# Weighted values of an attention block: the hi and lo weights moved in one 512-column matmul, with a sum of three pieces on VectorE

## The chip, the cores and the metric

The kernel runs on one core of one Trainium2 chip. The metric is the device time of one execution in microseconds (us). The engines are named as in the profile: PE is TensorE, with PEld for its weight loads, DVE is VectorE, ACT is ScalarE, POOL is GpSimd and SP is SyncE, which issues the DMAs.

## What is computed

One decoder layer over 1024 tokens of width 1024: half a SwiGLU feed-forward block (inner width 2816), a token mixer, and half a second feed-forward block, each behind an RMS norm and added to x, then a final norm. The change lies in the mixer, which has 8 stick-breaking heads and 8 dilated sliding-window heads of size 64:

```python
# stick-breaking head
z = q @ k.T * scale; mask = key < query
log_stay = where(mask, log_sigmoid(-z), 0)
later = reverse_cumsum(log_stay) - log_stay
weights = where(mask, exp(log_sigmoid(z) + later), 0)
out = weights @ v
# dilated head: softmax over z in each pattern, patterns mixed by their denominators, then weights @ v
```

What matters here is the last product, weights times v, of all 16 heads. All of it is float32.

## The kernel before, in words

**Precision.** Every float32 operand of a large product is split in two: hi is the value rounded to the reduced format in which PE takes float32 data (F32R), lo is what the rounding left. A product is then hi·hi + hi·lo + lo·hi. ACT writes the hi parts (a copy into an F32R tile) and DVE or POOL the lo parts (value minus hi).

**The stages.** `ffn_block` (first feed-forward), `heads_block` (projections and attention), `output_block` (the mixer's output projection) and `ffn_block` again. The change is in `heads_block` alone.

**The heads block.** It works in runs: four pairs of heads (`PAIRS`), and for each first the stick-breaking kind (`SB_KIND`) and then the dilated kind (`DIL_KIND`), eight runs in all. A run has 8 steps s: step s works on head s // 4 of the pair and on query group g = s % 4, which is 256 queries (`QG`). Group g looks at keys up to its own last one, so it has 2(g + 1) key tiles of 128. Runs sit in a loop on each engine (`Fori`) for the first three pairs; the last pair is written out, and its last run has no projection work beside it, because there is no further pair to project.

**What each engine does in a step.** The order on each engine is written out by hand in its `step` function:
- PE: the scores of the next step (`scores`, L1130 to L1161, into four PSUM banks); then, for each turn j of g + 1, some units of the next pair's projections (`project`, L1124 to L1126, as many as the table `UNITS` says), the transposes of the weights of two key tiles (`turn_weights`, L1180, into one bank of two), and the weighted values of the turn that lies two turns back (`values_behind` and `weighted_values`, L1194 to L1208).
- ACT: gates or exponentials (L819, L820, L829) of the next step, the hi part of the turned weights (`weights_hi`, L846), and where a step's values are complete, the copy of their lower half into `o_low` (`values_low`, L886). It also takes projections out of their bank (L861, L863, L867).
- DVE: scans or masked maxima (L956, L968), the normalising of the dilated weights (`normalize`, L981 and L983), the lo part of the turned weights (`weights_lo`, L997), rotations (L1032, L1035, L1041), and `values_out` (L1015).
- POOL: the stick-breaking products (`products`, L739), which end the making of a step's weights for that kind, one part of the rotations, and lo parts of the projection weights.

**The weighted values.** `v_both` holds for each key tile and head 128 columns: 64 with the hi part of v, 64 with the lo part. They are PE's stationary operand, so a matmul gives 128 rows: v_hi·w in rows 0 to 63 and v_lo·w in rows 64 to 127. Each key tile takes two matmuls with the same stationary operand and the same output columns of bank 4 (`BANK_PV`), one with `wt_hi` (L1206) and one with `wt_lo` (L1207). Both move 256 columns, except for the last key tile of a group, of which only 128 queries look at it, so that both move 128. Over all runs there are 256 tiles of the first kind and 64 of the second.

**How the bank is handed back.** There is one bank for it. When the last matmul of step s is done (`pv_ready`), ACT copies rows 64 to 127 of the bank into `o_low` (L886), DVE adds `o_low` to rows 0 to 63 and writes the sum into `o_stage` (L1015), in partitions 0 to 63 for the first head of the pair and 64 to 127 for the second. Only then (`o_copied`) may PE start the weighted values of step s + 1:

```python
if j == 0:
    pe.wait_ge(o_copied, 1 + STEPS * run(it, kind) + s)     # L1200
...
dve.wait_ge(o_low_done, STEPS * run(it, kind) + s + 1)      # L1014
dve.tensor_tensor(o_stage[rows, g * QG:(g + 1) * QG], b.ps[0:HEAD, BANK_PV, 0:QG], o_low[:, :],
                  ALU.add).then_inc(o_copied, 1)            # L1015
```

There are 64 such hand-backs. On DVE, `values_out` of a step stands between `weights_lo` and the scan or the masked maximum for the step after next (L1059 to L1065). In steps with g = 1 it stands there twice: once for the step with g = 3 before, once for the step with g = 0.

Of the kernel before, what the change touches and what calls it, by code (L numbers as in the profile page):

```python
# [30 lines left out]
P = 128  # L31
# [552 lines left out]
def heads_block(nc, b, sem, norm, w_in, neg_mask, log_count, cos, sin, o_dram, w_out, group_gain):  # L584
# [3 lines left out]
    with ExitStack() as ctx:  # L588
# [5 lines left out]
        cos_sb, sin_sb = sb("cos", [P, SEQ]), sb("sin", [P, SEQ])  # L594
        log_count_sb = sb("log_count", [P, SEQ])
        neg_f = sb("neg_f", [P, P])
        wt_hi = sb("wt_hi", [P, TT, QG], F32R)
        wt_lo = sb("wt_lo", [P, TT, QG], F32R)
        o_stage = sb("o_stage", [P, SEQ])
        w_raw, w_hi, w_lo = [b.w_raw[:, i, :, :] for i in range(2)], b.w_hi, b.w_lo  # L600

# [26 lines left out]
        turned, turn_hi_done, turn_split = sem("turned"), sem("turn_hi_done"), sem("turn_split")  # L628
        out_w_loaded = [sem(f"out_w_loaded{i}") for i in range(2)]
        out_w_hi_done, out_w_gained, out_w_split = (sem(f"out_w_{n}") for n in ("hi_done", "gained", "split"))  # L630
        pv_ready, o_low_done, o_copied = sem("pv_ready"), sem("o_low_done"), sem("o_copied")
        o_stored = [sem(f"o_stored{h}") for h in range(2)]
        block = ctx.enter_context(nc.Block())

# [13 lines left out]
        def run(it, kind):  # L648
            return 2 * it + kind
# [299 lines left out]
        def _(dve):  # L949
# [58 lines left out]
            def values_out(it, kind, s):  # L1008

                head, g = s // 4, s % 4  # L1010
                rows = slice(head * HEAD, (head + 1) * HEAD)
                if g == 0:
                    dve.wait_ge(o_stored[head], 16 * (run(it, kind) + 1))
                dve.wait_ge(o_low_done, STEPS * run(it, kind) + s + 1)  # L1014
                dve.tensor_tensor(o_stage[rows, g * QG:(g + 1) * QG], b.ps[0:HEAD, BANK_PV, 0:QG], o_low[:, :],  # L1015
                                  ALU.add).then_inc(o_copied, 1)

# [91 lines left out]
        def _(pe):  # L1109
# [84 lines left out]
            def weighted_values(it, kind, s, j, v_turn):  # L1194


                head, g = s // 4, s % 4
                pe.wait_ge(turn_split, 1 + TURNS * run(it, kind) + turn_index(s, j, v_turn) + 1)
                if j == 0:
                    pe.wait_ge(o_copied, 1 + STEPS * run(it, kind) + s)  # L1200
                for kk in range(2):
                    k, part = 2 * j + kk, wt_part(s, j) + kk
                    end = k == 2 * g + 1
                    cols = slice(P, QG) if end else slice(0, QG)
                    out, v = b.ps[:, BANK_PV, cols], v_both[kind][:, k, head, :]
                    pe.matmul(out, v, wt_hi[:, part, cols], start=(k == 0), stop=False)  # L1206
                    last = pe.matmul(out, v, wt_lo[:, part, cols], start=False, stop=end)  # L1207
                last.then_inc(pv_ready, 1)  # L1208

            def values_behind(it, kind, s, j, n):  # L1210
# [393 lines left out]
```

## Time and profile before

| | us |
|---|---|
| median of 3 executions | 2274.57 |
| lowest, highest | 2273.68, 2276.44 |
| span of the profiled execution, first to last instruction | 2270.4 |
| PE busy in it | 2185.7 |
| DVE busy in it | 996.2 |
| ACT busy in it | 658.7 |
| POOL busy in it | 215.3 |

The profile comes from one execution of its own, of which it states the span and not the whole time; the median of the runs stands 4.2 us above that span. Busy times are unions of instructions on an engine. A matmul's record is longer than the time it holds the engine, since matmuls overlap in the pipeline: what one costs is read from the start of one to the start of the next. In rows of a timeline, the bracket at the end gives the engine's idle time in front of the instruction and what ended it.

### The profile page before, as it was taken

To read this page: it belongs to the slowest core of one execution; us is meant where nothing else is said; L and a number is where in the kernel's file an instruction comes from. 1 tells how busy PE (TensorE), PEld (TensorE's weight loads), DVE (VectorE), ACT (ScalarE), POOL (GpSimd) and SP (SyncE) were. 2 spreads that over 40 slices of the span, in tenths; PEclk is the share of its full clock that TensorE was granted. 3 is DMA by queue.
4 is the path that set the end of the run, shared out by engine and by line. 5 is a ranking of instruction groups with operands and counts; after the bars stand their busy time and mean duration, and the time that the engine had idled before them with its cause. 6 is when DMAs were issued, how large, how long until landed. Compare 5 with 4: busy or idle time off the path is not lost. (4 is left out here: it accounts for less than half of the span.)

```text
span 2270.4 us, 26317 instructions
## 1 busy us (share of the span) xinstructions
PE 2185.7 (96%) x10016; PEld 1785.8 (79%) x10016; DVE 996.2 (44%) x1578; ACT 658.7 (29%) x1143; POOL 215.3 (9%) x138
## 2 busy tenths in 40 slices
PE   7999999999999899999999997799999999999998
PEld 6888888888887677777777776687888888888887
DVE  4233333332334446566565656343333333333236
ACT  5211111111112344554544545332211111111112
POOL 0000000000000032141241235300000000000000
PEclk9999999999999999999989986899999999999999
DMA  4111110111110301010110112402111111011101
GB/s 168 56 56 55 55 45 11 55 55 55 56 38 28 111 25 43 15 49 31 30 39 23 33 38 66 171 1 84 56 56 56 55 55 55 4 51 55 56 19 74
DMA packets 37960, 118.51 MB, mean 52 GB/s; under 512 B 4865, under 2 KB 9217, under 8 KB 37889
## 3 DMA queue, kind: packets, MB, share of 16 engines
q1 hardware_dynamic: 37888, 117.61, 14.5%
q8 instruction: 40, 0.66, 0.1%
q14 instruction: 32, 0.25, 0.0%
HBM read 100.81 MB, written 12.58 MB: 50 GB/s over the span
## 5 line engine op out<-in xcount | busy, mean ns | idle before, releaser
L360 DVE TENSOR_TENSOR scaled_rows<-banks,scaled_rows 128x512 f32<-128x512 f32 x88 | 60.9, 692 | 665.4 <-PE banks L435 511.4
L997 DVE TENSOR_TENSOR heads_wt_lo<-banks,heads_wt_hi 128x512 fp32r<-128x512 f32 (+2 forms) x224 | 105.3, 495 | 190.0 <-ACT heads_wt_hi L846 189.7
L1124 PE MATMUL banks<-first_hi,w_hi 128*128 128x512 f32 x384 | 165.1, 430 | 5.0 <-ACT heads_rot_in L867 2.9
L1125 PE MATMUL banks<-first_lo,w_hi 128*128 128x512 f32 x384 | 157.5, 410 | 0.0
L1126 PE MATMUL banks<-first_hi,w_lo 128*128 128x512 f32 x384 | 157.2, 409 | 0.0
L345 DVE SCALAR_TENSOR_TENSOR x_second<-banks,x_second 128x512 f32<-128x512 f32 x176 | 118.5, 689 | 74.0 <-PE banks L470 73.9
L345 DVE SCALAR_TENSOR_TENSOR x_first<-banks,x_first 128x512 f32<-128x512 f32 x176 | 117.8, 688 | 71.2 <-PE banks L470 71.2
L746 POOL TENSOR_TENSOR w_lo<-w_raw,w_hi 128x1024 fp32r<-128x1024 f32 x22 | 52.4, 2384 | 933.0 <-ACT w_hi L810 933.0
L846 ACT ACTIVATE heads_wt_hi<-banks 128x512 fp32r<-128x512 f32 (+2 forms) x224 | 93.2, 447 | 164.4 <-PE banks L1180 164.0
L468 PE MATMUL banks<-ffn_lo,ffn_hi 128*128 128x512 f32 x352 | 138.0, 392 | 1.2 <-DVE x_first L345 1.1
L433 PE MATMUL banks<-first_hi,w_hi 128*128 128x512 f32 x352 | 137.1, 390 | 1.2 <-DVE w_lo L325 1.2
L469 PE MATMUL banks<-ffn_lo,ffn_hi 128*128 128x512 f32 x352 | 137.7, 391 | 0.0
L470 PE MATMUL banks<-ffn_lo,ffn_hi 128*128 128x512 f32 x352 | 137.6, 391 | 0.0
L468 PE MATMUL banks<-first_lo,first_hi 128*128 128x512 f32 x352 | 137.0, 389 | 0.0
L433 PE MATMUL banks<-first_hi,ffn_lo 128*128 128x512 f32 x352 | 137.0, 389 | 0.0
L433 PE MATMUL banks<-second_hi,w_hi 128*128 128x512 f32 x352 | 137.0, 389 | 0.0
L433 PE MATMUL banks<-second_hi,first_lo 128*128 128x512 f32 x352 | 137.0, 389 | 0.0
L434 PE MATMUL banks<-first_lo,w_hi 128*128 128x512 f32 x352 | 137.0, 389 | 0.0
L435 PE MATMUL banks<-first_hi,ffn_lo 128*128 128x512 f32 x352 | 136.9, 389 | 0.0
L435 PE MATMUL banks<-second_hi,w_lo 128*128 128x512 f32 x352 | 136.9, 389 | 0.0
L435 PE MATMUL banks<-first_hi,w_lo 128*128 128x512 f32 x352 | 136.9, 389 | 0.0
L469 PE MATMUL banks<-first_lo,first_hi 128*128 128x512 f32 x352 | 136.9, 389 | 0.0
(139 smaller groups left out, 4687.3 us busy)
## 6 DMA issues: line engine op xcount, KB each, us to landing
w_raw<-in_ffn_w_gate SPq DMA_DIRECT2D x44, 512.0 KB, 6.9
ffn_up_raw<-in_ffn_w_up SPq DMA_DIRECT2D x44, 512.0 KB, 6.7
ffn_down_raw<-in_ffn_w_down SPq DMA_DIRECT2D x22, 1024.0 KB, 5.0
w_raw<-in_w_in SPq DMA_DIRECT2D x24, 512.0 KB, 3.9
x_first<-in_x SPq DMA_DIRECT2D x8, 512.0 KB, 6.7
x_between<-x_first SPq DMA_DIRECT2D x8, 512.0 KB, 2.6
heads_rot_swap<-heads_rot_in SPq DMA_DIRECT2D x64, 64.0 KB, 2.0
o_between<-heads_o_stage SPq DMA_DIRECT2D x16, 256.0 KB, 2.9
```

The costliest lines, as they stand in the source:

```text
L345: dve.scalar_tensor_tensor(out=b.x[:, t, cols], in0=b.ps[:, BANK_Y + g % 4, :], scalar=0.5, in1=b.x[:, t, cols], op0=ALU.mult, op1=ALU.add ...
L433: pe.matmul(b.ps[:, bank, :], hi[:, k, :], norm.xn_hi[:, k, cols], start=(k == 0), stop=False)
L434: pe.matmul(b.ps[:, bank, :], hi[:, k, :], norm.xn_lo[:, k, cols], start=False, stop=False)
L435: last = pe.matmul(b.ps[:, bank, :], lo[:, k, :], norm.xn_hi[:, k, cols], start=False, stop=(k == KT - 1))
L468: pe.matmul(out, h_hi[k][:, f, tok], w_hi[:, f, cols], start=(f == 0), stop=False)
L469: pe.matmul(out, h_hi[k][:, f, tok], w_lo[:, f, cols], start=False, stop=False)
L470: last = pe.matmul(out, h_lo[k][:, f, tok], w_hi[:, f, cols], start=False, stop=(f == CH - 1))
L846: last = act.activation(dst, b.ps[:, bank, cols], ACT.Copy)
L997: last = dve.tensor_tensor(dst, b.ps[:, bank, cols], hi.bitcast(F32), ALU.subtract)
L1124: pe.matmul(out, hi[:, k, :], norm.xn_hi[:, k, cols], start=(k == 0), stop=False)
L1125: pe.matmul(out, hi[:, k, :], norm.xn_lo[:, k, cols], start=False, stop=False)
L1126: last = pe.matmul(out, lo[:, k, :], norm.xn_hi[:, k, cols], start=False, stop=(k == KT - 1))
```

## The change

The two weight buffers become one, in which the hi and the lo part of each key tile lie next to each other (`wt_hi` and `wt_lo` are now views of it). One matmul moves both parts: 512 columns, or two pieces of 128 for the last key tile of a group. The hi part's products land in columns 0 to 255 of bank 4 and the lo part's in columns 256 to 511. DVE then adds columns 256 to 511 of rows 0 to 63 to `o_low`, waits for that on a new semaphore (`o_low_sum`), and makes the former sum. The product of v_lo and the lo weights, in rows 64 to 127 of the second half, is not added any more (before, it was part of `o_low`).

```diff
-        wt_hi = sb("wt_hi", [P, TT, QG], F32R)
-        wt_lo = sb("wt_lo", [P, TT, QG], F32R)
+        wt_both = sb("wt_both", [P, TT, 2, QG], F32R)
+        wt_hi, wt_lo = wt_both[:, :, 0, :], wt_both[:, :, 1, :]
...
-        pv_ready, o_low_done, o_copied = sem("pv_ready"), sem("o_low_done"), sem("o_copied")
+        pv_ready, o_low_done, o_low_sum, o_copied = (
+            sem("pv_ready"), sem("o_low_done"), sem("o_low_sum"), sem("o_copied"))
...
                 dve.wait_ge(o_low_done, STEPS * run(it, kind) + s + 1)
+                dve.tensor_tensor(o_low[:, :], b.ps[0:HEAD, BANK_PV, QG:2 * QG], o_low[:, :], ALU.add
+                                  ).then_inc(o_low_sum, 1)
+                dve.wait_ge(o_low_sum, STEPS * run(it, kind) + s + 1)
                 dve.tensor_tensor(o_stage[rows, g * QG:(g + 1) * QG], b.ps[0:HEAD, BANK_PV, 0:QG], o_low[:, :],
                                   ALU.add).then_inc(o_copied, 1)
...
                     cols = slice(P, QG) if end else slice(0, QG)
-                    out, v = b.ps[:, BANK_PV, cols], v_both[kind][:, k, head, :]
-                    pe.matmul(out, v, wt_hi[:, part, cols], start=(k == 0), stop=False)
-                    last = pe.matmul(out, v, wt_lo[:, part, cols], start=False, stop=end)
+                    out = b.ps[:, BANK_PV, :].rearrange("p (n c) -> p n c", c=QG)[:, :, cols]
+                    last = pe.matmul(out, v_both[kind][:, k, head, :], wt_both[:, part, :, cols],
+                                     start=(k == 0), stop=end)
```

## Rows read from the trace of the kernel before

**Rows 1.** The page: granted TensorE clock in 40 slices of the span, in tenths.

```profile
PEclk9999999999999999999989986899999999999999
```

**Rows 2.** Busy time by stretch: the heads block, then its last run (a dilated one).

```profile
804.00:1428.00 624.00, 586.49 (x2912) 463.62 (x2911) 380.59 (x745) 313.83 (x648) 189.22 (x115) 0.91 0.12 35
...
1372.00:1430.00 58.00, 44.87 (x180) 38.10 (x178) 34.88 (x83) 28.03 (x57) 30.09 (x14) 0.59 0.20 63
```

**Rows 3.** PE's groups by line and form: busy us, mean ns | idle before, releaser.

```profile
L1180 PE MATMUL banks<-ident_sb,scaled_rows 128*128 128x128 f32 x576 | 104.4, 306 | 20.1 <-POOL scaled_rows L739 12.0 <-DVE scaled_rows L983 8.0
L1206 PE MATMUL banks<-heads_wt_hi,heads_v_both 128*128 128x256 f32 x256 | 90.3, 366 | 10.9 <-DVE heads_o_stage L1015 10.9
```

**Rows 4.** PE's timeline: start us, us, what. Weighted values, then projections.

```profile
1099.83 0.28 PE L1207 MATMUL banks<-heads_wt_lo,heads_v_both 128*128 128x256 f32 x1
...
1100.18 0.40 PE L1124 MATMUL banks<-first_hi,w_hi 128*128 128x512 f32 x1
1100.42 0.39 PE L1125 MATMUL banks<-first_lo,w_hi 128*128 128x512 f32 x1
...
1102.01 0.39 PE L1126 MATMUL banks<-first_hi,w_lo 128*128 128x512 f32 x1
```

**Rows 5.** PE's timeline: the two matmuls of a last key tile, and the next one.

```profile
1102.91 0.22 PE L1206 MATMUL banks<-heads_wt_hi,heads_v_both 128*128 128x128 f32 x1
1102.97 0.27 PE L1207 MATMUL banks<-heads_wt_lo,heads_v_both 128*128 128x128 f32 x1
1103.08 0.45 PE L1124 MATMUL banks<-first_hi,w_hi 128*128 128x512 f32 x1
```

**Rows 6.** PE's timeline in a stretch of half the granted clock.

```profile
991.28 0.41 PE L1206 MATMUL banks<-heads_wt_hi,heads_v_both 128*128 128x256 f32 x1
991.50 0.41 PE L1207 MATMUL banks<-heads_wt_lo,heads_v_both 128*128 128x256 f32 x1
...
993.03 0.63 PE L1125 MATMUL banks<-first_lo,w_hi 128*128 128x512 f32 x1
993.46 0.63 PE L1126 MATMUL banks<-first_hi,w_lo 128*128 128x512 f32 x1
```

**Rows 7.** DVE's and PE's timeline: a stick-breaking hand-back of step 3.

```profile
1017.72 0.69 DVE L997 TENSOR_TENSOR heads_wt_lo<-banks,heads_wt_hi 128x512 fp32r<-128x512 f32 x1 [3.29 <-ACT heads_wt_hi L846]
1018.33 0.41 DVE L1015 TENSOR_TENSOR heads_o_stage<-banks,heads_o_low 64x256 f32<-64x256 f32 x1
...
1018.79 0.39 PE L1206 MATMUL banks<-heads_wt_hi,heads_v_both 128*128 128x256 f32 x1 [1.21 <-DVE heads_o_stage L1015]
```

**Rows 8.** DVE's and PE's timeline: a dilated hand-back of step 5.

```profile
1103.50 0.69 DVE L997 TENSOR_TENSOR heads_wt_lo<-banks,heads_wt_hi 128x512 fp32r<-128x512 f32 x1 [0.94 <-ACT heads_wt_hi L846]
1104.22 0.42 DVE L1015 TENSOR_TENSOR heads_o_stage<-banks,heads_o_low 64x256 f32<-64x256 f32 x1
...
1104.70 0.39 PE L1206 MATMUL banks<-heads_wt_hi,heads_v_both 128*128 128x256 f32 x1 [0.38 <-DVE heads_o_stage L1015]
...
1106.12 0.51 PE L1124 MATMUL banks<-first_hi,w_hi 128*128 128x512 f32 x1 [0.69 <-ACT heads_v_feature_major L861]
```

**Rows 9.** DVE's timeline: two instructions, the second waiting for the first.

```profile
1106.15 0.15 DVE L981 RECIPROCAL heads_row_inv<-heads_row_sum 128x1 f32<-128x1 f32 x1
1106.34 0.69 DVE L983 TENSOR_SCALAR scaled_rows<-scaled_rows,heads_row_inv 128x896 f32<-128x896 f32 x1
```

**Rows 10.** DVE's and PE's timeline: a stick-breaking hand-back of step 6.

```profile
1043.73 0.42 DVE L1015 TENSOR_TENSOR heads_o_stage<-banks,heads_o_low 64x256 f32<-64x256 f32 x1
...
1044.38 0.36 PE L1206 MATMUL banks<-heads_wt_hi,heads_v_both 128*128 128x256 f32 x1
```

**Rows 11.** PE's timeline: a wait for POOL's products.

```profile
1025.32 0.90 PE L1180 MATMUL banks<-ident_sb,scaled_rows 128*128 128x128 f32 x3 [0.45 <-POOL scaled_rows L739]
```

**Rows 12.** DVE's group at L1015, by form.

```profile
L1015 DVE TENSOR_TENSOR heads_o_stage<-banks,heads_o_low 64x256 f32<-64x256 f32 x64 | 26.4, 412 | 2.7 <-ACT heads_o_low L886 1.7
```

**Rows 13.** Busy time by stretch, around one fall of the granted clock.

```profile
990.00:997.00 7.00, 6.47 (x22) 5.20 (x22) 2.61 (x6) 2.61 (x7) 1.70 (x2) 0.51 0.25 68
```

## The prediction

> **What bounds the kernel now.** I read the page first. TensorE's granted clock stands at nine tenths or more nearly everywhere; the one place where it is lower is past the middle [rows 1]. The busy times by stretch narrow this: the heads block is the 624 us from 804 to 1428, PE is busy for 586 of them at a mean granted clock of 0.91, and its last run has a clock of 0.59 [rows 2]. So in most of the block PE is the engine that must not be held up, and what counts is how much each edit gives PE and how long PE is made to wait.
>
> Then PE's groups, for what ends its idle time. PE sat idle for 10.9 us in front of the weighted values, all of it until DVE's `values_out`, and for 20.1 us in front of the weights' transposes, until POOL's products or DVE's normalising [rows 3]. So the hand-back of bank 4 is already one of the waits that PE meets. The timeline shows how tight it is. In stick-breaking step 3, `values_out` ends at 1018.74 and PE starts at 1018.79: the smallest distance that occurs is 0.05 to 0.06 us, and PE had been idle for 1.21 us [rows 7]. I went through the 64 hand-backs in this way, from the end of L1015 to the next L1206, and took 0.056 us (0.148 at the lower clock) off each distance; the rest is what PE has to spare.
>
> **The matmuls: a gain.** Before, three steps of 256 columns take from 1099.83 to 1100.18, 0.117 us each, and seven steps of 512 columns from 1100.42 to 1102.01, 0.227 us each [rows 4]. A full key tile thus goes from 0.233 to 0.227 us, and 256 of them give 1.6 us. A last key tile takes 0.06 + 0.11 = 0.17 us for its two 128-column matmuls [rows 5]; one of 256 columns takes 0.117, so 64 of them give 64 x 0.053 = 3.4 us. That the 256 columns come in two pieces of 128 is a form without a row; it is bounded by the 0.117 of one piece and by 0.17, no gain. I take 0.117, because the columns moved are the same. Together 5.0 us at full clock. At half clock a 256-column step takes 0.22 us and a 512-column step 0.43 [rows 6], so full tiles give nothing there; and what is gained in front of a wait that DVE or POOL ends is lost in it. I take three quarters: 3.8 us, bounds 2 and 5.
>
> Here the Trainium skill would size it otherwise. "TensorE: Matmul & The Clock Gate", section "Back-to-back issue gap", gives 134, 262 and 518 cycles for 128, 256 and 512 columns: two small matmuls then cost only 6 cycles more than one twice as long, for either kind of tile. An estimate from it is 320 x 2.5 ns = 0.8 us for the whole gain. The trace disagrees for last tiles (0.17 against 0.117 us), so the sum keeps the rows' value.
>
> **The layout: nothing.** ACT and DVE now write their halves with a stride between key tiles, in instructions of the same size (L997, 0.69 us [rows 7]). This is hidden by the two turns that PE works between a turn's transposes and its weighted values; without that cover, each 0.01 us more in L997 would delay a turn by as much. Bounds: no gain, and 1 us in all.
>
> **The added instruction: a loss.** It has the shape of L1015, 412 ns [rows 12]. The second add waits for it; a DVE instruction that waits for the one before starts 0.04 us after its end (1106.30 to 1106.34) [rows 9]. So a hand-back gets 0.45 us longer where the head is the pair's first. For the second head, L1015 starts 0.03 us after `weights_lo` ends [rows 8], while for the first head it starts 0.08 us before [rows 7]. These two differ in the partitions written, and the new first add writes partitions 0 to 63 in both cases, like the latter. I therefore take 0.45 - 0.11 = 0.34 us for the second head (bounds 0.34 and 0.45).
>
> The Trainium skill ("VectorE: DVE Perf Modes", section "Two Vector instructions with no wait between them") says that an instruction is held until all earlier ones end if its output starts in another quadrant of partitions than the last output did. The 0.03 us after and 0.08 us before agree with it. The section "The DRAIN you can't avoid" says that a semaphore between two instructions costs nothing extra; by that, the second add would start early too, and the cost be 0.34 and 0.23 us.
>
> **Which of the 64 take it.** One pair of runs, from 973 to 1130; pairs 1 and 3 repeat it.
> - PE already waits (nothing to spare): stick-breaking (SB) steps 1, 3 and 5, dilated (DIL) step 5; [rows 7, 8] show two of them. SB 1 and 3: 0.45 each. SB 5: 0.34.
> - Little to spare: SB 6 (1044.15 to 1044.38, so 0.18) [rows 10], SB 7 and DIL 7 0.07 each, DIL 3 0.19, DIL 6 0.18. They pass on 0.16, 0.27, 0.27, 0.26 and 0.16.
> - DIL 5 is taken back: 1.4 us later PE waits 0.69 us for ACT to empty the projection bank [rows 8], and ACT's chain to that does not pass through the delayed matmuls. Nothing.
> - The other seven have 0.5 us or more to spare. Nothing.
> - Behind `values_out` on DVE stand the scans, whose results POOL multiplies and PE then transposes. Mostly this wait moves by as much as PE does. But two instructions (of SB 3 and SB 4) stand ahead of the scan that ends PE's wait of 0.45 us at 1025.32 [rows 11], and PE is late by only one: 0.34 more.
>
> A pair comes to 0.90 + 0.34 + 0.16 + 0.27 + 0.27 + 0.26 + 0.16 + 0.34 = 2.7 us; three pairs to 7.8 (the first has no DIL 7 ahead). The fourth pair's SB run: 0.27 + 0.45 + 0.45 + 0.34 + 0.34 + 0.16 + 0.34 = 2.35. Its DIL run has no projections, and there PE waits for DVE nearly all the time, so all of steps 1, 2, 3, 5, 6 and 7 pass it on: 3 x 0.45 + 3 x 0.34 = 2.4. Loss in all 12.5 us. DVE's added load of 64 x 0.45 = 29 us bounds nothing by itself, at 381 us busy of 624 [rows 2]. No DMA or other queue is moved; SP's store of a head starts up to 0.45 us later and is waited for only at the block's end (counted with step 7).
>
> **The sum.** +12.5 - 3.8 = +8.7 us. Against the profile's own span that is 2270.4 to 2279.1; the median of the runs lies 4.2 above that span, and I forecast 2274.6 + 8.7 = 2283.3. Its own range: high, 0.45 at every step, nothing taken back and a gain of 2 gives 17.6 - 2, 2290; low, half of the loss absorbed and the full gain gives 6.3 - 5, 2276.
>
> **Rivals.**
> - *The hand-back's added time stays hidden and the gain of the matmuls is left (faster).* For it: PE meets other waits, 20.1 us of them [rows 3], that could swallow a delay. Against it: those on POOL and L983 are themselves fed by DVE behind `values_out`. It needs less than 3.8 of the 12.5 us to come through, so that fewer than about 10 hand-backs decide. Time 2270.8. Chance 0.08.
> - *About half is absorbed.* 6.3 - 3.8 gives 2277. Chance 0.14.
> - *More stretches at half clock.* The granted clock falls to half, 1.2 GHz, for stretches of up to 7 us in the SB runs; this one [rows 13] begins right after PE had waited for POOL's products. Longer waits could add such a stretch. A 512-column step goes from 0.23 to 0.43 us [rows 4, 6], so 7 us of it cost up to 3.4. One more in each pair adds 13.6 to the forecast, 2297; two in all, 2290. Speaking against: in the DIL runs of the first three pairs PE waits little. Chance 0.14.
> - *The matmuls give only what the skill's cycle counts say.* From rows this is the case in which a last tile still takes its 0.17 us, with a gain of 1.2 us: 2285.9. Chance 0.04.
> - Forecast: 0.60.
>
> **Numbers.** About 0.2% (4.5 us) is what a measurement of this kernel can tell from no change. Slower by more: nearly all of the forecast, the clock and the cycle counts, and a little of the half case, 0.80. Within: 0.15. Faster: 0.05. The range reaches from the half case, 2276, to two more slow stretches beyond the forecast, 2292.
>
> **What would show it.** Right: 320 matmuls at the one remaining line, 0.227 us from start to start, 0.117 for a last tile; 64 more DVE instructions of about 412 ns; the same distance of 0.056 us from the second add to PE at SB 1, 3 and 5; SB 6 and 7 and DIL 3, 6 and 7 newly waiting; idle time in front of the weighted values up from 10.9 to some 20 us; a pair taking about 158.8 us instead of 157.0. Wrong: a pair no longer than before, a last tile at 0.17 us, or granted clock and not waits carrying the difference.

## The result, and the profile after

The changed kernel took 2282.10 us (median of 4 runs, 2278.20 to 2284.93) against 2275.19 for the kernel before: a ratio of 1.0036 [1.0021, 1.0051]. Run again beside 26 runs of before, 11 runs gave 2279.83 against 2274.08, 1.0025 [1.0013, 1.0037]. So it is slower by 6 to 8 us; 8.7 were forecast. It is not slower by a lower clock: the mean granted clock was 0.9685 and 0.9690 in its two sets of runs, 0.9677 to 0.9684 in those of the kernel before. The profiled execution took 2278.2 us for a span of 2276.4; the profiled spans differ by 6.0. Executions of one kernel scatter by several us (before: 2270.94 to 2281.10 over all runs, around 2274), so single spans can't be compared to better than that.

The groups of the heads block, from 804 to 1440, kept apart by form (PE's first, then DVE's):

```profile
L1210 PE MATMUL banks<-heads_wt_both,heads_v_both 128*128 128x512 f32 x256 | 108.0, 485 | 22.8 <-DVE heads_o_stage L1019 21.1 <-DVE heads_wt_both L998 0.4
L1184 PE MATMUL banks<-ident_sb,scaled_rows 128*128 128x128 f32 x576 | 102.7, 302 | 18.3 <-POOL scaled_rows L740 10.6 <-DVE scaled_rows L984 7.6
...
L1019 DVE TENSOR_TENSOR heads_o_stage<-banks,heads_o_low 64x256 f32<-64x256 f32 x64 | 26.7, 417 | 2.2
L1016 DVE TENSOR_TENSOR heads_o_low<-banks,heads_o_low 64x256 f32<-64x256 f32 x64 | 26.0, 406 | 1.2 <-ACT heads_o_low L887 1.1
...
L1210 PE MATMUL banks<-heads_wt_both,heads_v_both 128*128 128x256 f32 x64 | 19.1, 298 | 0.0
```

Where PE had sat idle for 10.9 us in front of the weighted values [rows 3], it now sits for 21.1; in front of the transposes it is 18.3 instead of 20.1. There are 256 + 64 matmuls at the one line that is left, and 64 more adds of 406 ns.

The hand-back of stick-breaking step 3, the answer to [rows 7], in DVE's and PE's timeline (start us, us, what, idle before it):

```profile
1018.21 0.69 DVE L998 TENSOR_TENSOR heads_wt_both<-banks,heads_wt_both 128x512 fp32r<-128x512 f32 x1 [3.28 <-ACT heads_wt_both L847]
1018.82 0.41 DVE L1016 TENSOR_TENSOR heads_o_low<-banks,heads_o_low 64x256 f32<-64x256 f32 x1
1019.26 0.42 DVE L1019 TENSOR_TENSOR heads_o_stage<-banks,heads_o_low 64x256 f32<-64x256 f32 x1
...
1019.73 0.62 PE L1210 MATMUL banks<-heads_wt_both,heads_v_both 128*128 128x512 f32 x2 [1.79 <-DVE heads_o_stage L1019]
```

From the start of the first add to PE it took 0.46 us (1018.33 to 1018.79) and takes 0.91 (1018.82 to 1019.73): 0.45 longer. The dilated step 5, the answer to [rows 8]:

```profile
1103.47 0.69 DVE L998 TENSOR_TENSOR heads_wt_both<-banks,heads_wt_both 128x512 fp32r<-128x512 f32 x1 [0.94 <-ACT heads_wt_both L847]
1104.08 0.41 DVE L1016 TENSOR_TENSOR heads_o_low<-banks,heads_o_low 64x256 f32<-64x256 f32 x1
1104.52 0.42 DVE L1019 TENSOR_TENSOR heads_o_stage<-banks,heads_o_low 64x256 f32<-64x256 f32 x1
...
1104.99 0.73 PE L1210 MATMUL banks<-heads_wt_both,heads_v_both 128*128 128x512 f32 x2 [0.82 <-DVE heads_o_stage L1019]
...
1106.09 0.50 PE L1128 MATMUL banks<-first_hi,w_hi 128*128 128x512 f32 x1 [0.37 <-ACT heads_v_feature_major L862]
```

Here the first add starts 0.08 us before `weights_lo` ends (1104.08 against 1103.47 + 0.69) instead of 0.03 after it. From that end to PE it is 0.83 us instead of 0.51: 0.32 longer. And the wait for ACT behind it fell from 0.69 to 0.37 us, so this step costs nothing, as announced.

What the matmuls gave is best read from a turn with a last key tile, in PE's timeline:

```profile
1102.56 0.59 PE L1210 MATMUL banks<-heads_wt_both,heads_v_both 128*128 128x512 f32 x2
1102.98 0.40 PE L1128 MATMUL banks<-first_hi,w_hi 128*128 128x512 f32 x1
```

That turn, a full key tile and a last one, takes 0.42 us from 1102.56; before, the same one took 0.49, from 1102.59 to the projection at 1103.08 [rows 5]. Over all turns at full clock the medians are 0.431 against 0.489 us for a turn with a last tile and 0.546 against 0.556 for two full tiles. The 64 and 96 turns of the block would make 3.7 + 1.0 = 4.7 us at full clock.

Where the distances to the next weighted values had been small, they are used up. Step 6, which had 0.18 us to spare [rows 10], now starts 0.05 us after the second add:

```profile
1043.73 0.42 DVE L1019 TENSOR_TENSOR heads_o_stage<-banks,heads_o_low 64x256 f32<-64x256 f32 x1
1044.20 0.73 PE L1210 MATMUL banks<-heads_wt_both,heads_v_both 128*128 128x512 f32 x2
```

### The profile page after: what moved, and what is told of

Same layout as the page of the kernel before. It is cut to its first block and busy times, and to the rows that moved or that the text cites. A ratio compares the mean times of both kernels' runs of the same rounds, so it can differ in the third digit from the quotient of the medians.

```text
span 2276.4 us, 25741 instructions
## 1 busy us (share of the span) xinstructions
PE 2181.0 (96%) x9696; PEld 1760.5 (77%) x9696; DVE 1014.4 (45%) x1642; ACT 659.6 (29%) x1143; POOL 215.8 (9%) x138
## 5 line engine op out<-in xcount | busy, mean ns | idle before, releaser
L998 DVE TENSOR_TENSOR heads_wt_both<-banks,heads_wt_both 128x512 fp32r<-128x512 f32 (+2 forms) x224 | 105.2, 495 | 175.1 <-ACT heads_wt_both L847 174.7
L1130 PE MATMUL banks<-first_hi,w_lo 128*128 128x512 f32 x384 | 156.4, 407 | 0.0
L847 ACT ACTIVATE heads_wt_both<-banks 128x512 fp32r<-128x512 f32 (+2 forms) x224 | 93.1, 446 | 158.0 <-PE banks L1184 157.7
L1210 PE MATMUL banks<-heads_wt_both,heads_v_both 128*128 128x512 f32 x320 | 116.3, 448 | 22.8 <-DVE heads_o_stage L1019 21.1
L434 PE MATMUL banks<-second_lo,w_hi 128*128 128x512 f32 x352 | 137.6, 391 | 0.0
L468 PE MATMUL banks<-first_lo,first_hi 128*128 128x512 f32 x352 | 137.2, 390 | 0.0
L433 PE MATMUL banks<-first_hi,ffn_lo 128*128 128x512 f32 x352 | 137.2, 390 | 0.0
L433 PE MATMUL banks<-second_hi,first_lo 128*128 128x512 f32 x352 | 137.2, 390 | 0.0
L435 PE MATMUL banks<-second_hi,first_lo 128*128 128x512 f32 x352 | 137.1, 389 | 0.0
```

Source lines behind the costliest of these rows:

```text
L433: pe.matmul(b.ps[:, bank, :], hi[:, k, :], norm.xn_hi[:, k, cols], start=(k == 0), stop=False)
L434: pe.matmul(b.ps[:, bank, :], hi[:, k, :], norm.xn_lo[:, k, cols], start=False, stop=False)
L435: last = pe.matmul(b.ps[:, bank, :], lo[:, k, :], norm.xn_hi[:, k, cols], start=False, stop=(k == KT - 1))
L468: pe.matmul(out, h_hi[k][:, f, tok], w_hi[:, f, cols], start=(f == 0), stop=False)
L998: last = dve.tensor_tensor(dst, b.ps[:, bank, cols], hi.bitcast(F32), ALU.subtract)
L1130: last = pe.matmul(out, lo[:, k, :], norm.xn_hi[:, k, cols], start=False, stop=(k == KT - 1))
```

## DVE's scans took back a part

One step of the prediction was that POOL's wait in front of step 6's transposes [rows 11] grows by 0.34, since two adds stand ahead of that scan on DVE. It did not:

```profile
1026.28 1.11 PE L1184 MATMUL banks<-ident_sb,scaled_rows 128*128 128x128 f32 x4 [0.44 <-POOL scaled_rows L740]
```

DVE's timeline shows why. Before, between the hand-backs of steps 3 and 4 and the scan that follows:

```profile
1018.65 1.53 DVE L956 TENSOR_TENSOR_SCAN heads_stay<-heads_stay 128x640 f32<-128x640 f32 x1
...
1021.21 1.99 DVE L956 TENSOR_TENSOR_SCAN heads_stay<-heads_stay 128x768 f32<-128x768 f32 x1
1023.12 0.66 DVE L1032 TENSOR_TENSOR heads_rot_swap<-heads_rot_swap,heads_sin 128x512 f32<-128x512 f32 x1
```

and after:

```profile
1019.60 1.47 DVE L957 TENSOR_TENSOR_SCAN heads_stay<-heads_stay 128x640 f32<-128x640 f32 x1
...
1022.40 1.76 DVE L957 TENSOR_TENSOR_SCAN heads_stay<-heads_stay 128x768 f32<-128x768 f32 x1
1024.07 0.67 DVE L1036 TENSOR_TENSOR heads_rot_swap<-heads_rot_swap,heads_sin 128x512 f32<-128x512 f32 x1
```

The big scan starts 1.19 us later but takes 0.23 less, so what follows is only 0.95 later, which is PE's own delay. The difference is POOL, in its timeline before and after:

```profile
1020.26 1.32 POOL L739 TENSOR_TENSOR scaled_rows<-scaled_rows,heads_stay 128x640 f32<-128x640 f32 x1 [1.43 <-DVE heads_stay L956]
```

```profile
1021.15 1.32 POOL L740 TENSOR_TENSOR scaled_rows<-scaled_rows,heads_stay 128x640 f32<-128x640 f32 x1 [1.81 <-DVE heads_stay L957]
```

Before, POOL's product of the last scan runs until 1021.58, 0.37 us into the scan that starts at 1021.21; after, until 1022.47, 0.07 into the one from 1022.40. Scans of this size take 1.74 us with no product beside them, 1.99 with 0.38 us of one and 2.25 with 0.64, over all that the two traces hold. Later scans miss the products. Their groups, in the kernel before, in the changed one and in the one with a third add (below):

```profile
L956 DVE TENSOR_TENSOR_SCAN heads_stay<-heads_stay 128x1024 f32<-128x1024 f32 x8 | 22.5, 2814 | 0.1
L956 DVE TENSOR_TENSOR_SCAN heads_stay<-heads_stay 128x768 f32<-128x768 f32 x8 | 16.9, 2115 | 0.1
```

```profile
L957 DVE TENSOR_TENSOR_SCAN heads_stay<-heads_stay 128x1024 f32<-128x1024 f32 x8 | 20.1, 2507 | 0.1
L957 DVE TENSOR_TENSOR_SCAN heads_stay<-heads_stay 128x768 f32<-128x768 f32 x8 | 14.2, 1771 | 0.1
```

```profile
L959 DVE TENSOR_TENSOR_SCAN heads_stay<-heads_stay 128x1024 f32<-128x1024 f32 x8 | 18.3, 2282 | 0.1
L959 DVE TENSOR_TENSOR_SCAN heads_stay<-heads_stay 128x768 f32<-128x768 f32 x8 | 14.0, 1748 | 0.1
```

So the added 26 us of adds came with 5 us less of scans. The Trainium skill has this rule ("SBUF — State Buffer", section "Who interferes with whom"): a VectorE instruction with two SBUF inputs contends with a GpSimd instruction that reads SBUF. The scans agree with it.

## The experiments

The theory after the result: the two adds in the hand-back cost, the matmuls give a little back. Rivals: that PE's waits elsewhere swallow one or the other, or that VectorE's load as such counts, wherever the add stands. Each figure below is the median time and the ratio to the kernel before on the same chip, with its 95% interval; a difference in us is worked out from the ratio.

**The matmuls apart again.** The changed kernel, its matmul split in two that write the same two halves:

```diff
-                    last = pe.matmul(out, v_both[kind][:, k, head, :], wt_both[:, part, :, cols],
-                                     start=(k == 0), stop=end)
+                    v = v_both[kind][:, k, head, :]
+                    pe.matmul(out[:, 0, :], v, wt_hi[:, part, cols], start=(k == 0), stop=False)
+                    last = pe.matmul(out[:, 1, :], v, wt_lo[:, part, cols], start=False, stop=end)
```

> The changed kernel with each 512-column matmul taken apart again into two (hi weights into columns 0 to 255 of the bank, lo weights into columns 256 to 511); the sum of three pieces stays. Theory (the added hand-back time costs, the merged matmuls give some 3.8 us back): slower than the changed kernel by 2 to 5 us, so 11 to 13 us above the kernel before, near 2287, PE idle in front of the weighted values again some 21 us, a last key tile at 0.17 us. Rival 1 (the merge gives only 0.8 to 1.2 us): about 1 us above the changed kernel, 2283. Rival 2 (what differs is carried by stretches of the lower TensorE clock): no fixed order to the changed kernel, the stretches differ in number.

2289.61 us, 1.0060 [1.0036, 1.0084], +13.7. The direction is as expected and the size a little above the 11 to 13 expected. A turn with a last key tile is back at 0.491 us and one of two full tiles at 0.558 (medians at full clock, 0.489 and 0.556 in the kernel before), as expected; PE's wait for the bank is 18.1 us and not 21. But the runs scatter from 2280.6 to 2296.1, and the trace has a wait that belongs to no theory, ahead of PE's first matmuls of a turn of the loop over pairs:

```profile
977.57 0.71 PE L1160 MATMUL banks<-heads_k_hi,heads_q_hi 64*128 64x512 f32 x1 [3.32 <-issue]
```

PE waited there for no semaphore; the queue that the profile marks as carrying instructions (q8) moved 49 packets instead of 39, and between 830 and 1285 us, inside the loop, 14 instead of 5. So up to 3.3 us of the 13.7 are not the matmuls' time.

**The third piece left out.** The first add and its wait go (the output then lacks the product of v's high part with the weights' low part):

```diff
-                dve.tensor_tensor(o_low[:, :], b.ps[0:HEAD, BANK_PV, QG:2 * QG], o_low[:, :], ALU.add
-                                  ).then_inc(o_low_sum, 1)
-                dve.wait_ge(o_low_sum, STEPS * run(it, kind) + s + 1)
```

> The merged matmuls with the hand-back of before: VectorE makes one add, so that the product of v_hi with the lo weights is left out of the output. Theory: the matmul gain alone, 3.8 us (bounds 2 and 5) below the kernel before, near 2271.4; PE idle in front of the weighted values about 11 us as before; a ratio of 0.998. Rival 1 (cycle counts): 0.8 us, no difference from before. Rival (the gain is lost in waits that VectorE and GpSimd end): within 1 us of before although the matmuls are shorter.

2272.35 us, 0.9989 [0.9979, 0.9998]: -2.5 us (-4.8 to -0.5). This is what the matmuls' gain alone brings in the total; 3.8 had been taken. PE's wait for the bank is 13.1 us, where about 11 had been expected. (The first difference and this one don't agree: taking the matmuls apart cost 6.8 us, merging them gave 2.5. The wait above is up to 3.3 of that; the rest is open.) Against the average of the two comparisons of the changed kernel (1.0030, +6.9 us), the added instruction costs some 9.4 us; 12.5 had been taken.

**A third add**, to a spare tile, between the two:

```diff
+                dve.tensor_tensor(o_spare[:, :], b.ps[0:HEAD, BANK_PV, QG:2 * QG], o_low[:, :], ALU.add
+                                  ).then_inc(o_spare_sum, 1)
+                dve.wait_ge(o_spare_sum, STEPS * run(it, kind) + s + 1)
```

> The changed kernel with one more add of the same shape at each hand-back (into a spare tile, with its own semaphore), so 0.45 us more once again. Theory: every hand-back that PE now waits for passes it on: per pair nine steps of 0.45 and two smaller parts, 4.5 us; three pairs and the last pair's 6 us make 18 to 20 us over the changed kernel, near 2301. Rival (most of a longer hand-back is absorbed by other waits): under 9 us over it, below 2291. Rival (clock): the difference stands in more stretches at half clock than the changed kernel has, and not in idle time before the weighted values.

2294.62 us, 1.0078 [1.0064, 1.0093], +17.7, some 11 above the changed kernel's +6.9; the second add had cost 9.4. That lies between the theory (18 to 20) and its rival (under 9). The mean granted clock of the runs is 0.9693, no lower than before. PE's waits in the block, from its trace (us in total, times, longest):

```profile
PE banks L1215 <- DVE heads_o_stage L1024: 35.6, 39, 2.2
PE banks L1189 <- DVE scaled_rows L986: 7.5, 4, 3.0
PE banks L1189 <- POOL scaled_rows L742: 7.5, 9, 1.6
```

Idle in front of the weighted values goes 10.9, 21.1, 35.6 us, that for POOL's products 12.0, 10.6, 7.5: each add is met in more places (17, 22, 39 times) and takes a little off the other wait.

**The bank handed back early.** On the kernel before: DVE copies rows 0 to 63 out while ACT copies the others, PE waits for the two copies only, and the sum (now of two SBUF tiles) is off its path.

```diff
+            def values_read(it, kind, s):
+                dve.wait_ge(pv_ready, 4 + BANKS * run(it, kind) + bank_count(s + 1))
+                dve.wait_ge(o_copied, 1 + STEPS * run(it, kind) + s)
+                dve.tensor_copy(o_high[:, :], b.ps[0:HEAD, BANK_PV, 0:QG]).then_inc(bank_read, 1)
...
-                    pe.wait_ge(o_copied, 1 + STEPS * run(it, kind) + s)
+                    pe.wait_ge(bank_read, 1 + STEPS * run(it, kind) + s)
+                    pe.wait_ge(o_low_done, 1 + STEPS * run(it, kind) + s)
```

> The kernel before (two matmuls per key tile) with the bank handed back earlier: VectorE copies rows 0 to 63 out of the bank while ScalarE copies rows 64 to 127, ahead of the lo part of the turned weights in VectorE's queue, and the sum is made from the two copies off PE's path. Theory (the hand-back is what PE waits for): the chain is 0.4 us shorter at every step, so PE's 10.9 us in front of the weighted values shrink to those of stick-breaking steps 1 and 3, where ScalarE is late, some 5 us; 4 to 8 us faster than before, 2267 to 2271. Rival (the waits behind take it up): PE's idle time moves to the transposes and the projections and the time is within 2 us of before. Rival (VectorE's one more instruction delays scans): slower by 1 to 4 us.

2279.71 us, 1.0017 [1.0007, 1.0027]: slower, where a gain was expected. The theory that a shorter hand-back is time won did not hold in this form. PE's waits of that kernel:

```profile
PE banks L1192 <- POOL scaled_rows L741: 17.9, 12, 2.0
PE banks L1192 <- DVE scaled_rows L986: 10.4, 5, 4.2
PE banks L1136 <- ACT heads_v_feature_major L863: 6.8, 7, 1.3
PE banks L1168 <- issue: 4.7, 2, 2.5
PE banks L1219 <- ACT heads_o_low L889: 1.9, 3, 0.7
```

The wait for the bank is nearly gone (1.9), but what DVE took on ahead of its scans comes back through POOL (12.0 to 17.9), L983's successor (8.0 to 10.4) and the projection bank (2.1 to 6.8). And 4.7 us are waits of the other kind, with 23 packets on q8 in the loop, 18 more than before. The next kernel replaces PE's two waits by one on a semaphore that ACT and DVE both count up:

```diff
+                    pe.wait_ge(bank_free, 2 * (1 + STEPS * run(it, kind) + s))
```

> The early copy again, but ScalarE and VectorE both count up one semaphore, so that PE's program has no more waits than before. In the first form PE's program had one more wait in each step, and the trace showed instruction fetches on DMA queue 8 all through the loop and PE idle for 2.2 to 2.5 us right after the loop's turn. Theory (fetching the longer loop again cost some 5 us of the 3.9 us loss): no fetches in the loop beyond those of before, 5 us faster than the first form, 2274 to 2276, about as before. Rival (VectorE's additional instruction ahead of the scans costs what the shorter hand-back gives, and the fetches nothing): 2279 to 2280 again. Rival (the hand-back is all that counts): 2267 to 2271.

2276.71 us, 1.0007 [0.9997, 1.0017]. As expected there is no wait on issue and q8 moves 5 packets in the loop, as before. The kernel is 2 to 3 us faster than the first form, where 5 had been expected, and level with before. The two largest of PE's waits are now:

```profile
PE banks L1191 <- POOL scaled_rows L741: 21.9, 12, 2.5
PE banks L1191 <- DVE scaled_rows L986: 13.5, 5, 4.5
```

**The changed kernel handed back early**, DVE summing the bank's halves with one reduce and adding ACT's part later:

```diff
+                dve.tensor_reduce(o_high[:, :], b.ps[0:HEAD, BANK_PV, :].rearrange("p (n c) -> p c n", c=QG),
+                                  mybir.AxisListType.X, ALU.add).then_inc(bank_free, 1)
```

> The merged matmuls with an early hand-back: VectorE sums the two halves of rows 0 to 63 out of the bank in one reduce of 512 elements (about 0.7 us), beside ScalarE's copy, ahead of the lo part of the turned weights; the last sum is made off PE's path; one semaphore for PE. Theory (PE waits for the bank less than in the changed kernel, VectorE's load is 0.3 us larger at each step): PE idle in front of the weighted values under 8 us instead of 22, but the scans are later by as much as in the changed kernel or more, so 3 to 7 us faster than the changed kernel, 2275 to 2279. Rival (load ahead of the scans is what counts): no faster than the changed kernel, 2281 to 2286.

2280.58 us, 1.0031 [1.0018, 1.0043]: no faster than the changed kernel, though PE's wait for the bank fell to 3.8 us, under the 8 expected. The reduce took 679 ns, the sum 550 in the mean, and PE's wait for POOL was 22.2 us.

In all three early forms the sum has two SBUF tiles as inputs. It takes 404 to 422 ns where no POOL instruction runs beside it (41, 42 and 46 of the 64 in the three traces), just as an add out of the bank does, and else mostly 0.5 to 1.3 us, in single cases 1.4 to 2.5. Its means are 625, 613 and 550 ns. So these kernels also put a collision with POOL into DVE's queue, ahead of the scans, and a form without one was not run.

**Where the time counts, 1: behind the hand-back.** The kernel without the third piece, with an instruction on DVE that no other engine waits for, behind `values_out` and ahead of the scan:

```diff
+                dve.wait_ge(o_spare_done, 1 + STEPS * run(it, kind) + s)
+                dve.tensor_tensor(o_spare[:, :], cos_sb[0:HEAD, 0:300], sin_sb[0:HEAD, 0:300], ALU.add
+                                  ).then_inc(o_spare_done, 1)
```

> The kernel without the third piece (merged matmuls, hand-back of before) with one more VectorE instruction of about 0.4 us behind each values_out, of data that nobody needs: VectorE's load is that of the changed kernel, the hand-back is not longer. Theory (PE's wait for the bank is what costs): it delays only the scans behind it, PE's waits for products grow by some 0.4 us at two or three places of a pair, so 3 to 6 us above the kernel without the third piece (2276 to 2279) and clearly below the changed kernel. Rival (it is VectorE's load ahead of the scans and not the hand-back that costs): the time of the changed kernel, 2282 to 2284. Rival (neither: the scans have room): within 2 us of 2272.4.

2288.57 us, 1.0049 [1.0032, 1.0066], more than either theory gave. But the instruction had been meant to take about 0.4 us, and took 642 ns in the mean. With 180 columns it took 499:

```profile
L1021 DVE TENSOR_TENSOR heads_o_spare<-heads_cos,heads_sin 64x180 f32<-64x180 f32 x64 | 31.9, 499 | 1.0
```

> As the kernel with the additional VectorE instruction behind values_out (f2), but with 180 columns in place of 300: in f2 that instruction took 0.64 us instead of the 0.4 meant, and the kernel lay 13.7 us above the one without the third piece. Now some 0.4 us. Theory (every 0.4 us that stands ahead of the scans costs about as much as a longer hand-back does, because the scans, the products on GpSimd and the transposes make a chain of their own): 2278 to 2282, 6 to 9 us above the kernel without the third piece. Rival (the chain over the scans has room for 0.4 us and not for 0.64): within 3 us of that kernel, 2273 to 2276.

2280.04 us, 1.0027 [1.0015, 1.0038]: as slow as the changed kernel and within the theory's range, though PE's wait for the bank has not grown at all (12.0 us against 13.1 without the instruction). Its waits:

```profile
PE banks L1186 <- POOL scaled_rows L742: 16.2, 12, 2.2
PE banks L1212 <- DVE heads_o_stage L1018: 12.0, 16, 1.4
PE banks L1186 <- DVE scaled_rows L986: 9.2, 4, 3.8
```

Against the kernel without it, PE's idle time in front of the transposes rises from 20.6 to 25.4 us (9 of these waits are put down to POOL there and 3, of 4.2 us, to DVE's `heads_v_both`; here 12 to POOL, 16.2), and that in front of the projections from 4.4 to 6.1. So DVE's time counts behind the hand-back too, through other waits.

How much a given time counts there, this does not show, for two reasons. The 499 ns are a mean of unlike cases:

```profile
L1021 DVE TENSOR_TENSOR heads_o_spare<-heads_cos,heads_sin x64: 327/339/2340, 817.1 to 1433.9; 64x180 f32<-64x180 f32 x64
```

These are minimum, median and maximum. The instruction reads two SBUF tiles; 44 of the 64 have no POOL instruction beside them and take at most 340 ns, while in stick-breaking step 1 it takes 1.22 us beside POOL's product. And the granted clock was lower: 0.9649 in the mean of the seven runs, against 0.9682 for the kernel before beside them (0.9653 against 0.9677 for the longer instruction). What that is worth stands below.

**Where the time counts, 2: in the hand-back, but not on DVE.** The kernel without the third piece, with ACT's copy made twice (0.42 us more before DVE may start):

```diff
+                act.activation(o_spare[:, :], b.ps[HEAD:P, BANK_PV, 0:QG], ACT.Copy).then_inc(o_spare_done, 1)
+                act.wait_ge(o_spare_done, STEPS * run(it, kind) + s + 1)
```

> The kernel without the third piece, in which ScalarE's copy into o_low is made twice, one after the other (0.42 us more in the hand-back, VectorE not busier). VectorE's queue is held at values_out for that time. Theory (the delay counts and not the busy time of VectorE): as the changed kernel, 2279 to 2283, PE idle in front of the weighted values above 20 us. Rival (VectorE has idle time in front of values_out or the delay is hidden behind weights_lo, which it executes meanwhile): 1 to 4 us above the kernel without the third piece, 2273 to 2276, PE idle there 14 to 17 us.

2279.10 us, 1.0028 [1.0018, 1.0038]: again as slow as the changed kernel, though DVE does no more work than without it. Its wait for the bank was 16.6 us, less than the 20 that the theory gave and nearer to the rival's; DVE, which now stands in front of the hand-back and waits (3.8 us in nine places), may pass part of the delay on to all that is queued behind; PE's idle time from 790 to 1460 rose by 8.0 us against the kernel without the third piece, 3.5 of them for the bank.

**The sum on POOL**, off DVE altogether, for the early copy and for the early reduce (`values_out` moves from DVE's queue to POOL's, with two buffers):

```diff
+                pool.tensor_tensor(o_stage[head][:, g * QG:(g + 1) * QG], o_high[s % 2][:, :], o_low[s % 2][:, :],
+                                   ALU.add).then_inc(o_copied, 1)
```

> The early copy with one semaphore (f3), but with the sum made on GpSimd, into a tile of its own for each head, and two buffers for each copy. The bank is handed back 0.4 us earlier than before, and VectorE has one instruction of 0.4 us at a step, as before. Theory (both the hand-back and VectorE's load count): faster than before by 3 to 8 us, 2266 to 2271. Rival (the wait for pv_ready ahead of weights_lo is what holds VectorE in f3): as f3, 2275 to 2277. Rival (GpSimd's sum delays its products, or slows VectorE): slower than f3, PE's waits for GpSimd over 22 us.

> The merged matmuls with the early reduce (f4) and the sum on GpSimd. VectorE has 0.3 us more at a step than before instead of 0.6. Theory: 3 to 6 us faster than f4 and than the changed kernel, 2274 to 2278. Rival (GpSimd's sum delays its products): no faster than f4, 2280 or more.

2293.30 us, 1.0083 [1.0069, 1.0097], and 2301.38, 1.0121 [1.0105, 1.0136]: the theory of both fell, the rival held. POOL takes 0.98 us for that add in the mean (median 0.73, longest 3.21) and 1.40 in the second, ahead of its products; PE's wait for these, in the first of the two (37.9 us in the second):

```profile
PE banks L1192 <- POOL scaled_rows L740: 31.5, 14, 3.0
```

**The changed kernel again**, in a batch with others:

> The changed kernel once more, as the measure for the others beside it. Theory: 8 us above the kernel before (6 to 11), as measured first.

Its numbers stand with the result: 1.0025 [1.0013, 1.0037], +5.7 us, just under the 6 to 11 expected; its wait for the bank is 22.3 us.

## Why the prediction was right, point by point

- *Slower by 8.7 us, range 2276 to 2292.* +6.9 in the two comparisons together, inside the range and within 2 us of the forecast. The rivals "stays hidden" (2270.8) and "more half-clock stretches" (2290 and up) did not happen: the mean granted clock from 804 to 1428 is 0.91 in both traces, and that of the runs is no lower. Both terms were taken too large, and it is luck that their errors partly cancel: a loss of 12.5 against 9.4, a gain of 3.8 against 2.5. The range's upper end was called two more slow stretches; by the prediction's own prices these give 2290, not 2292.
- *The matmuls.* Each price held: 0.431 us for a turn with a last tile and 0.546 for two full ones, a gain of 4.7 at full clock where the working had 5.0. Of the 0.058 us by which a turn with a last tile is shorter, some 0.005 are its full tile's, so an estimated 0.053 are the last tile's, as in the working. The Trainium skill's cycle counts ("TensorE: Matmul & The Clock Gate", section "Back-to-back issue gap"), by which the whole gain would be 0.8 us, do not hold for it. The section gives them for a matmul by itself and says that at 128 columns they are too low; its 81 ns for one in a stream fit the pair's 0.17 us, while its 131 ns for 512 columns do not fit the 0.227 us here. The share that comes through was taken too high: 2.5 of 4.7 (0.5 to 4.8), not three quarters.
- *The hand-back.* 0.45 and 0.34 were announced; 0.45 and 0.32 are there. PE's wait in step 3 rose by more, 0.58 us (1.21 to 1.79), as PE began it 0.13 us earlier against DVE's first add: so a gain in front of a wait is lost in it. The semaphore between the adds is not free: the second starts 0.035 us after the first's end, where the first starts 0.08 before the end of `weights_lo`. The Trainium skill's section "Two Vector instructions with no wait between them" ("VectorE: DVE Perf Modes") agrees with the first add; its section "The DRAIN you can't avoid", by which a semaphore costs nothing extra (it was measured there on a chain of copies), does not agree with the second.
- *Which of them take it.* Steps SB 6 and 7, DIL 3, 6 and 7 now stand at 0.05 us, and DIL 5 was taken back, as said. DIL 1, which was given half a microsecond to spare, stands at 0.05 too, though PE need not wait longer for it.
- *The wait for POOL, 0.34 more.* **This step failed**: 0.45 became 0.44 us. It had DVE's instructions at fixed durations. They are not; the scan behind got shorter by what it no longer overlaps with POOL. Four such terms are 1.4 us of the 12.5. Without them 11.1 are left, and PE's waits together did rise by 11.1 us (49.9 to 61.0, all that the traces hold from 790 to 1460); that this fits to a tenth is luck.
- *A pair would take 158.8 us.* **This sign failed** in the first trace of the changed kernel, where a pair took 157.0, as before, and not in the second, where the same one took 159.6 and the next 160.5. In that first trace PE is 2.3 us less busy in the pair, and the granted clock is 0.96 instead of 0.95. The execution of before had one more stretch at 1.2 GHz; in that place, before and after:

```profile
1038.00:1041.20 3.20, 3.20 (x12) 2.91 (x13) 1.19 (x4) 2.15 (x3) 0.00 (x0) 0.50 0.00 0
```

```profile
1038.00:1041.20 3.20, 2.13 (x12) 1.85 (x13) 1.50 (x3) 1.55 (x3) 0.94 (x1) 1.00 0.00 0
```

Up to here after was 1.2 us behind (at step 7's transposes), and 0.2 us ahead where the dilated run starts. At the end of the block it is 4.6 us behind (the output block starts at 1441.85 instead of 1437.27), and in the second trace 7.2 (1444.46). So one trace per kernel can't say how the loss splits over the pairs; the runs say how large it is.

**The granted clock differs from kernel to kernel.** These are the windows of the second pair, from step 2's `values_out` to the next pair's (stretch, length, busy us of PE, PEld, DVE, ACT and POOL with their instructions, granted clock, DMA share, GB/s), for the kernel before, the two traces of the changed one, the one without the third piece, the same with the short instruction behind, and the early copy with one wait:

```profile
998.50:1155.51 157.01, 151.01 (x770) 118.86 (x769) 95.16 (x189) 78.87 (x164) 41.68 (x26) 0.95 0.12 34
999.59:1156.57 156.98, 148.66 (x689) 112.10 (x689) 99.69 (x204) 79.09 (x164) 41.71 (x26) 0.96 0.12 34
998.43:1158.05 159.62, 149.65 (x689) 113.35 (x688) 100.02 (x205) 79.25 (x164) 41.73 (x26) 0.95 0.11 33
999.47:1156.52 157.05, 150.36 (x689) 114.23 (x689) 94.69 (x190) 79.19 (x164) 41.67 (x26) 0.93 0.12 34
999.85:1158.29 158.44, 151.96 (x691) 115.97 (x690) 98.87 (x205) 79.36 (x164) 41.72 (x26) 0.92 0.12 33
999.72:1156.53 156.81, 148.24 (x770) 117.13 (x769) 101.39 (x206) 78.95 (x164) 41.72 (x26) 0.96 0.12 34
```

By the traces' record of the clock, 17.1, 13.7, 17.1, 20.5, 23.9 and 13.7 us of these were at 1.2 GHz, while PE was idle for 6.0, 8.3, 10.0, 6.7, 6.5 and 8.6. Without the third piece the pair has its shorter matmuls and hardly more waits, and takes 157.05 us all the same, at a lower clock. The runs say it too: their mean clock is 0.9673 without the third piece (before 0.9684), 0.9649 with the short instruction behind and 0.9666 with ACT's second copy (before 0.9682), but 0.9706 and 0.9712 for the two early copies (before 0.9684 and 0.9677). A thousandth is 4.6 us at half clock and so worth up to 2.3 us, by this estimate. For the kernel without the third piece that is up to 2.5 us, about its missing share of the gain; for the short instruction behind up to 7.5. What makes the clock differ is not shown.

**What the prediction had not seen** is the larger lesson. It treated the hand-back as the one place where the half microsecond counts. The early hand-backs and the instruction behind say otherwise. PE is fed by two chains that run through DVE's queue: the bank's hand-back, and scan, POOL's product, transpose. More time in the first cost 9 us for 0.45 (the second add) and for 0.42 (ACT's second copy). More time on DVE behind it cost 8.5 us for 0.5 in the mean, but that was unevenly laid and came with a lower clock, so that a price for the second chain is not shown. Taking the sum off the first chain and leaving it ahead of the second moves the wait (10.9 us for the bank to 2.7, 12.0 for POOL to 21.9) and adds to it: with the early copy and one wait PE was idle for 64.7 us from 790 to 1460 instead of 49.9. That this kernel is level with before goes together with less time at half clock, 128.0 us instead of 145.8 in the two traces. No variant that computes everything was faster than the kernel before; the closest, 2276.71 against 2274.08, is level within its interval.

**What stays open.** How much of the 13.7 us of the split matmuls is instruction fetching, since only one of its six runs was profiled. Why PE's idle time adds up to the difference in the spans only in some pairs of traces. For the first trace of the changed kernel, 11.1 more idle, less 4.7 for the matmuls and 3.4 for 6.8 us fewer at half clock (119.5 instead of 126.3 from 800 to 1460) would be 3, where 6 are measured. For the second, 13.8 more idle, less 4.7, with 126.3 at half clock, make 9.1, where 8.7 are measured. For the kernel without the third piece, 2.2 more idle, less 4.7, and 8.5 for 17.1 us more at half clock make 6.0, where 0.8 are measured; the half-clock stretches may lie partly in PE's waits, which was not followed up.

## What to carry to other kernels

Before a piece of work is put into a queue, count every chain that passes through that queue behind it, not only the one that waits for its result; the test is the same duration at the next place in the queue, where nothing waits for it. Such a test instruction must take the same time at every place: look at its shortest and longest case and not at its mean, and at the granted clock of the runs. Merging matmuls that move the same columns gives only what the smallest of them waste: here some 53 ns for a pair of 128 columns, 5 for a pair of 256, and that does not pay for 0.45 us on a chain that PE waits for.

## What the hardware did that was not expected

- PE can stand still at the turn of a loop while instructions are fetched. In three kernels (the early copy with two waits, the split matmuls, the early copy with its sum on POOL) PE had idle times of 2.2 to 3.3 us there that no semaphore ended, and in just these q8 moved more packets inside the loop, 9 for each such time, 49 or 58 in all instead of 39 or 40. In PE's timeline of the first (one of its two):

```profile
976.12 0.49 PE L1168 MATMUL banks<-heads_k_hi,heads_q_hi 64*128 64x512 f32 x1 [2.53 <-issue]
```

One wait fewer in each step removed it there, with 2 to 3 us. That the fetches cause the idle time is read from their falling together, and what makes a program need them is open: the split matmuls are as many as the kernel before has, where q8 moves only 5 packets in that time.

- An add of two SBUF tiles costs DVE no more than one with a PSUM input as long as POOL rests: 404 to 422 ns for 64x256, 327 to 340 for 64x180, 450 to 466 for 64x300, against 412 for 64x256 out of a bank. Beside an instruction of POOL one took up to 1.35 us in the first three pairs and up to 2.5 in the last, while the add out of the bank stays at 402 to 419 either way. A plain copy of 64x256 out of the bank takes 412 as well, so copying is no cheaper than adding. The scans' dependence on POOL's work, which is the same thing, is told above.
